# The first block's softmax: each component's negated maximum goes straight to its exponential, component 1 first

## The chip, the core and the metric

The kernel runs on one core of one Trainium2 chip. The metric is the device time of one execution in microseconds; the figure compared is the median of several runs. The engines are PE (TensorE, matmuls), DVE (VectorE), ACT (ScalarE), POOL (GpSimd) and SP, which here only issues the weight loads. They run side by side and wait for each other through semaphores.

## The reference

The program applies a first block and then a second block, each two layers deep, to x of 1024 tokens by 1024 features. Only the attention of the first block matters here. It has four heads; each head has two components c of 64 columns and one shared set of values of 128 columns. Rotation (RoPE) is applied to q and k.

```
q = q * (A_QK_DIM ** -0.5)
sc = jnp.einsum('bhcqd,bhckd->bhcqk', qi, kh)
p = jax.nn.softmax(jnp.where(mask, sc, NEG_INF), axis=-1)
w = p[:, :, 0] - lam * p[:, :, 1]
return jnp.einsum('bhqk,bhkv->bhqv', w, vh)
```

The result of a head is normalised (rms_norm), multiplied with silu(z), and later merged with a convolution branch and a retention branch. Queries are taken in blocks of 128, and block q of a head needs the keys 0 to 128(q+1).

## The kernel before, in words

Every engine has its own instruction stream, written out in the same order of steps; there is no scheduler. Attention of one layer (`attention` of each engine) runs over four heads h and eight query blocks q. The work of one block has these steps:

- PE `scores` (L728) computes both components' scores of 128 x 128(q+1) into the two buffers of psA; the last matmul of each component (L733) adds the causal mask and fills the buffer. It runs one block ahead, and may start when both buffers were drained by the exponentials of the block before.
- DVE `maxima` (L1274, L1275) takes the row maximum of each component and multiplies both with -SCALE (1/8), into `negmax`.
- ACT `exps` (L992) computes exp(SCALE * score + negmax) of each component into tiles 4 to 7 of X, which is free in that phase, with the row sum on the side; finishing it drains the score buffer.
- DVE `mix` (L1283 to L1285) takes the reciprocals of the sums, scales component 1 with its own and -lambda, and adds the scaled component 0.
- PE transposes the mixture (L706), ACT copies it (L1081), and PE multiplies it with the values (L778).

Between these, PE computes the projections of the next head (q, k, v, z, and in the last head the first panels of the convolution) as 24 matmuls of 128x512 for each half of the tokens (L483). These matmuls are most of PE's time in this phase. Each product is computed in three passes, with weights and activations split into a high and a low part; POOL splits each weight panel (L449, L452) once PE has begun the panel before.

Projections, transposes, rotations and the sum of squares of the head's output (L767) share three banks of psT in a ring called F. A step whose bank is still in use waits until the step three before it has been drained: q, k and v by ACT's copy (L1002), convolution panels by ACT's copy (L1011), the swapped q and k of the rotation by DVE's L1294, the sum of squares by ACT's logarithm (L1015). The order of each engine is fixed, so that L1002, L1011 and L1015 stand behind the exponentials of the next block on ACT, and L1294 behind the maxima of the next block on DVE. `B1_SLOTS` lists which step goes into which block; (("ss", 0, 0)) of block 6 puts L767 there, and ("v", 1, 1) of block 7 the projection that needs the bank of that sum.

`Ring` and `Tally` only count semaphores: `A.filled` is one semaphore for all of psA, counted in the order component 0, component 1; `A.drained` is one per buffer. `step` lets DVE wait for its own last instruction.

Of the kernel before, what the change touches and what calls it, by code (L numbers as in the profile page):

```python
# [19 lines left out]
ALU = mybir.AluOpType  # L20
ACT = mybir.ActivationFunctionType
AX_X = mybir.AxisListType.X
# [7 lines left out]
P = 128  # L30
SEQ, D_MODEL, DEPTH = 1024, 1024, 2
KT = D_MODEL // P
NT = SEQ // P
# [5 lines left out]
HEADS = 4  # L39
# [285 lines left out]
class C1:  # L325
# [5 lines left out]
    n = KT + 15  # L331


class C2:
# [13 lines left out]
    n = 100  # L348
# [3 lines left out]
class K:  # L352
# [11 lines left out]
    n = 896 + 1024 + 2  # L364
# [162 lines left out]
def first_block(env):  # L527
    nc, X, Hhi, Hlo, rope, ident, ones = env.nc, env.X, env.Hhi, env.Hlo, env.rope, env.ident, env.ones
    psA, psT, identb, maskb, epsc = env.psA, env.psT, env.identb, env.maskb, env.epsc
    SCALE = A_QK ** -0.5  # L530
    with ExitStack() as ctx:
        def sem(name):
            return env.sem("b1_" + name)

        def sb(name, shape, dt=F32):
            return ctx.enter_context(nc.sbuf_tensor("b1_" + name, shape, dt))
# [11 lines left out]
        lam = sb("lam", [P, 6])  # L548
# [1 line left out]
        swapa = sb("swapa", [P, P])  # L550
        swapr = sb("swapr", [P, P])
        rtab = sb("rtab", [P, K.n - K.dmask])
        rowmax = sb("rowmax", [P, 2])
        negmax = sb("negmax", [P, 2, 2])
        rowsum = sb("rowsum", [P, 2, 2])
        inv = sb("inv", [P, 2, 2])
# [4 lines left out]
        A = Ring("b1A", a_uses, env.sem)  # L561
# [3 lines left out]
        F = Ring("b1F", f, env.sem, 3)  # L565
# [8 lines left out]
        s, saved = env.s, env.saved  # L574
# [10 lines left out]
            sem(n) for n in ("sq2_done", "sq2_added", "summed2", "mean2", "root2", "both", "x_fin"))  # L585
        lam_sum, lam_exp = Tally(sem("lam_sum"), 1), Tally(sem("lam_exp"), 1)
        rotated = Tally(sem("rotated"), 4 * HEADS)
        nmax = Tally(sem("nmax"), HEADS * NT)
        mixed = Tally(sem("mixed"), HEADS * NT)
        a_sq, a_rs, a_out = (Tally(sem(n), 2 * HEADS) for n in ("a_sq", "a_rs", "a_out"))  # L590
        b_hi, b_lo = (Tally(sem(n), 2 * HEADS + 2 * B1_TILES) for n in ("b_hi", "b_lo"))
# [16 lines left out]
        TMP, ROT = upad[:, 2:2 + HALF], upad[:, 2 + HALF:]  # L608
# [364 lines left out]
        def scalar(act):  # L973
# [11 lines left out]
                act.activation(dst, psA[:, A.buf(use)], func).then_inc(A.freed(use), 1)  # L985

            def exps(L, h, q):
                act.wait_ge(*nmax.upto(L, h * NT + q + 1))
                n = (q + 1) * P
                for c in (0, 1):  # L990
                    use = ("s", h, q, c)
                    act.activation(PR[q % 2][c][:, 0:n], psA[:, A.buf(use), 0:n], ACT.Exp,  # L992
                                   bias=negmax[:, q % 2, c:c + 1], scale=SCALE,
                                   accum_out=rowsum[:, q % 2, c:c + 1]).then_inc(A.freed(use), 1)

            def piece(L, use):
# [259 lines left out]
        def vector(dve):  # L1256
            def step(ins):
                dve_step.step(dve, ins)
# [9 lines left out]

            def maxima(L, h, q):
                n = (q + 1) * P  # L1270
                for c in (0, 1):
                    use = ("s", h, q, c)
                    dve.wait_ge(*A.filled(L, use))
                    step(dve.reduce_max(rowmax[:, c:c + 1], psA[:, A.buf(use), 0:n], AX_X))  # L1274
                dve.tensor_scalar(negmax[:, q % 2], rowmax[:], -SCALE, None, ALU.mult).then_inc(nmax.sem, 1)  # L1275

            def mix(L, h, q):

                n = (q + 1) * P
                p0, p1 = PR[q % 2][0][:, 0:n], PR[q % 2][1][:, 0:n]  # L1280
                dve.wait_ge(*A.drained(L, ("s", h, q, 0)))
                dve.wait_ge(*A.drained(L, ("s", h, q, 1)))
                step(dve.reciprocal(inv[:, q % 2], rowsum[:, q % 2]))  # L1283
                step(dve.tensor_scalar(p1, p1, inv[:, q % 2, 1:2], lam[:, 4:5], ALU.mult, ALU.mult))
                dve.scalar_tensor_tensor(out=p0, in0=p0, scalar=inv[:, q % 2, 0:1], in1=p1, op0=ALU.mult, op1=ALU.add)\  # L1285
                    .then_inc(mixed.sem, 1)

            def piece(L, use):
                kind, h, half = use
                c, psF = slice(half * HALF, (half + 1) * HALF), bank(use)  # L1290
                if kind in ("sq", "sk"):
                    dst = (AQ if kind == "sq" else AK)[h % 2][:, c]
                    dve.wait_ge(*F.filled(L, use))
                    dve.tensor_tensor(ROT, psF, rope[:, 1, c], ALU.mult).then_inc(F.freed(use), 1)  # L1294
                    step(dve.tensor_tensor(dst, dst, rope[:, 0, c], ALU.mult))
                    dve.wait_ge(*F.drained(L, use))
                    dve.tensor_tensor(dst, dst, ROT, ALU.add).then_inc(rotated.sem, 1)
                    dve.wait_ge(*rotated.upto(L, rotations(h, kind[1], half)))
                elif kind == "vt":
                    dve.wait_ge(*F.filled(L, use))  # L1300
                    dve.tensor_copy(AVAL[h % 2][:, c], psF).then_inc(F.freed(use), 1)
                elif kind == "ss":
                    n = 2 * h + half
                    dve.wait_ge(*a_rs.upto(L, n + 1))
                    dve.scalar_tensor_tensor(out=TMP, in0=psAV, scalar=gcol[:, 0:1], in1=TMP, op0=ALU.mult,
                                             op1=ALU.mult).then_inc(AV.freed((h, half)), 1)
                    dve.wait_ge(*AV.drained(L, (h, half)))
                    dve.wait_ge(*F.drained(L, ("z", h, half)))
                    dve.tensor_tensor(TMP, TMP, Z[:, c], ALU.mult).then_inc(a_out.sem, 1)
# [1447 lines left out]
```

## Time and profile before

| | us |
|---|---|
| median of 3 runs | 3851.65 (3850.85 to 3853.29) |
| the profiled execution's own time | 3852.72 |
| its span | 3850.9 |
| PE busy | 3701.6 (96%) |
| DVE busy | 1759.4 (46%) |
| ACT busy | 1107.3 (29%) |
| POOL busy | 1408.3 (37%) |

Attention of the first block runs from about 88 to 415 us in the first layer, and from about 1265 to 1590 us in the second. In a row of a timeline stand the start, the duration, the engine, the line and the operation, what it writes and reads, and how many instructions were merged into the row; a bracket gives the idle time of the engine before it and the engine and line that ended it. In a row of the windows stand the stretch, its length, the busy time (and instructions) of PE, of PE's weight loads, of DVE, ACT and POOL, then the granted clock, the share of the DMA engines and GB/s. Granted clock is the share of full speed that TensorE was allowed. Line numbers are those of the kernel before; in the changed kernel the lines up to the maxima stand one lower, and in `mix` and `piece` they differ by up to three.

### The profile page before, as it was taken

To read this page: it belongs to the slowest core of one execution; us is meant where nothing else is said; L and a number is where in the kernel's file an instruction comes from. 1 tells how busy PE (TensorE), PEld (TensorE's weight loads), DVE (VectorE), ACT (ScalarE), POOL (GpSimd) and SP (SyncE) were. 2 spreads that over 40 slices of the span, in tenths; PEclk is the share of its full clock that TensorE was granted. 3 is DMA by queue.
4 is the path that set the end of the run, shared out by engine and by line. 5 is a ranking of instruction groups with operands and counts; after the bars stand their busy time and mean duration, and the time that the engine had idled before them with its cause. 6 is when DMAs were issued, how large, how long until landed. Compare 5 with 4: busy or idle time off the path is not lost.

```text
span 3850.9 us, 43042 instructions
## 1 busy us (share of the span) xinstructions
PE 3701.6 (96%) x16664; PEld 2832.3 (74%) x16664; DVE 1759.4 (46%) x2125; ACT 1107.3 (29%) x1819; POOL 1408.3 (37%) x734
## 2 busy tenths in 40 slices
PE   6999999999999999999999999999899999999999
PEld 5666788887778666788887787777666678766667
DVE  4555113223145655204213235882566579345654
ACT  3334100112212333210102212123455331435542
POOL 2212344343356222244442347442323255333324
PEclk9999999999999999999999999999899999999999
DMA  4000111111124100111111114311111231111122
GB/s 151 28 27 28 47 53 46 49 47 33 39 88 142 33 28 28 44 51 48 47 52 33 33 44 139 104 39 33 37 29 31 80 122 50 33 32 33 34 70 90
DMA packets 74684, 209.40 MB, mean 54 GB/s; under 512 B 8224, under 2 KB 13600, under 8 KB 74016
## 3 DMA queue, kind: packets, MB, share of 16 engines
q1 hardware_dynamic: 53712, 159.15, 14.0%
q10 hardware_dynamic: 20816, 48.01, 3.5%
q8 instruction: 118, 1.93, 0.2%
q14 instruction: 38, 0.31, 0.0%
HBM read 186.16 MB, written 20.97 MB: 54 GB/s over the span
## 4 chain that ended last, share of the span: by engine, by line
PE 88%; DVE 8%; ACT 3%; issue 1%; DMA 0%; SPq 0%; ACTq 0%; DVEq 0%
PE psA L502 45%; PE psT L483 17%; PE psA L483 7%; PE psA L1819 3%; PE psA L728 2%; PE psT L1886 2%; PE psT L778 2%; PE psT L1790 1%; PE psT L1795 1%; DVE b_rowmax L1274 1%; PE psT L1863 1%; ACT X L992 1%; PE psT L1860 1%; PE psT L706 1%; PE psT L700 1%
## 5 line engine op out<-in xcount | busy, mean ns | idle before, releaser
L449 POOL TENSOR_TENSOR Whi<-stage,credit 128x1024 fp32r<-128x1024 f32 (+2 forms) x364 | 600.6, 1650 | 2394.8 <-PE psA L502 1200.0
L452 POOL TENSOR_TENSOR Wlo<-stage,Whi 128x1024 fp32r<-128x1024 f32 (+2 forms) x364 | 807.4, 2218 | 28.6
L502 PE MATMUL psA<-Hhi,Whi 128*128 128x512 f32 x2240 | 702.6, 395 | 0.4 <-DVE b_ypad L2327 0.4
L502 PE MATMUL psA<-Hlo,Whi 128*128 128x512 f32 x2240 | 690.2, 389 | 0.0
L502 PE MATMUL psA<-Hhi,Wlo 128*128 128x512 f32 x2240 | 689.9, 389 | 0.0
L502 PEld LDWEIGHTS psA<-Hhi,Whi 128*128 128x128 f32 x2240 | 419.2, 188 | 101.3 <-issue 16.6
L502 PEld LDWEIGHTS psA<-Hlo,Whi 128*128 128x128 f32 x2240 | 420.5, 188 | 88.1
L502 PEld LDWEIGHTS psA<-Hhi,Wlo 128*128 128x128 f32 x2240 | 420.5, 188 | 88.1
L483 PE MATMUL psT<-Hhi,Whi 128*128 128x512 f32 x1024 | 426.9, 417 | 33.1 <-ACT b_upad L1015 15.0
L483 PE MATMUL psT<-Hhi,Wlo 128*128 128x512 f32 x1024 | 406.5, 397 | 0.0
L483 PE MATMUL psT<-Hlo,Whi 128*128 128x512 f32 x1024 | 406.5, 397 | 0.0
L483 PEld LDWEIGHTS psT<-Hhi,Whi 128*128 128x128 f32 x1024 | 197.6, 193 | 91.2 <-issue 51.3
L2337 DVE SCALAR_TENSOR_TENSOR b_wk<-b_ypad,b_cur,b_wk 128x1024 f32<-128x1024 f32 x120 | 230.5, 1921 | 4.1
L483 PEld LDWEIGHTS psT<-Hhi,Wlo 128*128 128x128 f32 x1024 | 196.7, 192 | 43.7
L483 PEld LDWEIGHTS psT<-Hlo,Whi 128*128 128x128 f32 x1024 | 197.6, 193 | 39.4 <-issue 3.2
L483 PE MATMUL psA<-Hhi,Whi 128*128 128x512 f32 x448 | 181.9, 406 | 7.2 <-DVE Hlo L1379 6.3
L483 PE MATMUL psA<-Hhi,Wlo 128*128 128x512 f32 x448 | 176.6, 394 | 0.0
L483 PE MATMUL psA<-Hlo,Whi 128*128 128x512 f32 x448 | 176.2, 393 | 0.0
L985 ACT ACTIVATE b_wk<-psA 128x1024 f32<-128x1024 f32 x44 | 45.1, 1026 | 443.1 <-PE psA L502 443.0
L1274 DVE TENSOR_REDUCE b_rowmax<-psA 128x1 f32<-128x256 f32 (+7 forms) x128 | 97.0, 757 | 165.2 <-PE psA L733 162.7
L1102 ACT ACTIVATE b_wk<-psA 128x1024 f32<-128x1024 f32 x32 | 32.9, 1027 | 440.8 <-PE psA L502 440.8
L1819 PE MATMUL psA<-b_wk 128*128 128x512 f32 (+3 forms) x384 | 149.4, 499 | 5.0 <-ACT b_wk L2076 4.5
(320 smaller groups left out, 4883.4 us busy)
## 6 DMA issues: line engine op xcount, KB each, us to landing
stage<-in_w SPq DMA_DIRECT2D x232, 512.0 KB, 3.5
stage<-in_w SPq DMA_DIRECT2D x68, 256.0 KB, 2.6
xs<-X ACTq DMA_DIRECT2D x8, 2048.0 KB, 8.0
stage<-in_w SPq DMA_DIRECT2D x32, 384.0 KB, 3.1
b_wk<-xs ACTq DMA_DIRECT2D x36, 256.0 KB, 5.2
rope<-in_ropes ACTq DMA_DIRECT2D x4, 1024.0 KB, 5.0
stage<-in_w SPq DMA_DIRECT2D x32, 128.0 KB, 2.1
X<-xs ACTq DMA_DIRECT2D x8, 512.0 KB, 8.1
```

What stands on the lines that cost most here:

```text
L449: pool.tensor_tensor(Whi[:, b, 0:n], stage[:, b, 0:n], credit[:, 0:1].broadcast_to([P, n]), ALU.add).then_inc(s.w_hi, 1)
L452: pool.tensor_tensor(Wlo[:, b, 0:n], stage[:, b, 0:n], Whi[:, b, 0:n].bitcast(F32), ALU.subtract).then_inc(s.w_split, 1)
L483: mm = pe.matmul(dst[0:M], w[:, cols], r[k][:, c], start=k == 0 and w is whi and r is rhi, stop=k == nk - 1 and end)
L502: mm = pe.matmul(dst[h], w[:, cols], r[k][:, h * HALF:(h + 1) * HALF], start=first and k == order[0] and r is rhi and w is whi, stop=last ...
L700: mm = pe.matmul(dst[:, c], lhsT, rhs[:, c], start=start, stop=stop)
L728: pe.matmul(dst[:, k0:k1], AQ[h % 2][rows, q * P:n], AK[h % 2][rows, k0:k1], start=True, stop=k1 < n)
L778: mm = pe.matmul(psAV[:, c0:], AVAL[h % 2][:, k * P:(k + 1) * P], WT[:, k, c0:], start=k == 0, stop=k == 4 * g + 3)
L985: act.activation(dst, psA[:, A.buf(use)], func).then_inc(A.freed(use), 1)
L1274: step(dve.reduce_max(rowmax[:, c:c + 1], psA[:, A.buf(use), 0:n], AX_X))
L1819: pe.matmul(dst[:, k0:k1], Q[sd][:, q * P:n], keys[g][:, 0:k1 - k0], start=True, stop=k1 < n)
L1886: mm = pe.matmul(psAV[side_rows(sd), c0:], v[:, b * M_V:(b + 1) * M_V], WT[sd][:, k, c0:], start=k == 0, stop=k == 4 * g + 3)
L2337: ins = dve.scalar_tensor_tensor(out=YC[:, t], in0=ypad[:, t, k:k + SEQ], scalar=col(C2.conv_w + 2 * k + t), in1=YC[:, t], op0=ALU.mult, o ...
```

## The change

`negmax` gets one maximum per component directly: the reduction is told to negate its result. The multiplication with SCALE moves from there and from the exponential to the rotation of q, whose two multiplications (by the sine and the cosine table) become scalar_tensor_tensor operations with SCALE as their constant; those of k get the same operations with 1.0. The tile `rowmax` and the instruction L1275 go. The semaphore `nmax` counts each component. Maxima and exponentials take component 1 first, and each exponential waits only for its own maximum. Both maxima wait until component 1's scores are filled, which come last. `mix` first waits for component 1, takes its reciprocal and scales it, and then waits for component 0 and takes that reciprocal by itself.

```diff
-        nmax = Tally(sem("nmax"), HEADS * NT)
+        nmax = Tally(sem("nmax"), 2 * HEADS * NT)
...
             def exps(L, h, q):
-                act.wait_ge(*nmax.upto(L, h * NT + q + 1))
                 n = (q + 1) * P
-                for c in (0, 1):
+                for c in (1, 0):
                     use = ("s", h, q, c)
+                    act.wait_ge(*nmax.upto(L, 2 * (h * NT + q) + 2 - c))
                     act.activation(PR[q % 2][c][:, 0:n], psA[:, A.buf(use), 0:n], ACT.Exp,
-                                   bias=negmax[:, q % 2, c:c + 1], scale=SCALE,
+                                   bias=negmax[:, q % 2, c:c + 1],
...
             def maxima(L, h, q):
                 n = (q + 1) * P
-                for c in (0, 1):
+                for c in (1, 0):
                     use = ("s", h, q, c)
-                    dve.wait_ge(*A.filled(L, use))
-                    step(dve.reduce_max(rowmax[:, c:c + 1], psA[:, A.buf(use), 0:n], AX_X))
-                dve.tensor_scalar(negmax[:, q % 2], rowmax[:], -SCALE, None, ALU.mult).then_inc(nmax.sem, 1)
+                    dve.wait_ge(*A.filled(L, ("s", h, q, 1)))
+                    dve.reduce_max(negmax[:, q % 2, c:c + 1], psA[:, A.buf(use), 0:n], AX_X, negate=True)\
+                        .then_inc(nmax.sem, 1)
...
             def mix(L, h, q):
-                dve.wait_ge(*A.drained(L, ("s", h, q, 0)))
-                dve.wait_ge(*A.drained(L, ("s", h, q, 1)))
-                step(dve.reciprocal(inv[:, q % 2], rowsum[:, q % 2]))
-                step(dve.tensor_scalar(p1, p1, inv[:, q % 2, 1:2], lam[:, 4:5], ALU.mult, ALU.mult))
+                dve.wait_ge(*A.drained(L, ("s", h, q, 1)))
+                step(dve.reciprocal(inv[:, q % 2, 1:2], rowsum[:, q % 2, 1:2]))
+                step(dve.tensor_scalar(p1, p1, inv[:, q % 2, 1:2], lam[:, 4:5], ALU.mult, ALU.mult))
+                dve.wait_ge(*A.drained(L, ("s", h, q, 0)))
+                step(dve.reciprocal(inv[:, q % 2, 0:1], rowsum[:, q % 2, 0:1]))
                 dve.scalar_tensor_tensor(out=p0, in0=p0, scalar=inv[:, q % 2, 0:1], in1=p1, op0=ALU.mult, op1=ALU.add)\
                     .then_inc(mixed.sem, 1)
...
                 if kind in ("sq", "sk"):
-                    dve.tensor_tensor(ROT, psF, rope[:, 1, c], ALU.mult).then_inc(F.freed(use), 1)
-                    step(dve.tensor_tensor(dst, dst, rope[:, 0, c], ALU.mult))
+                    scale = SCALE if kind == "sq" else 1.0
+                    dve.scalar_tensor_tensor(out=ROT, in0=psF, scalar=scale, in1=rope[:, 1, c], op0=ALU.mult,
+                                             op1=ALU.mult).then_inc(F.freed(use), 1)
+                    step(dve.scalar_tensor_tensor(out=dst, in0=dst, scalar=scale, in1=rope[:, 0, c], op0=ALU.mult,
+                                                  op1=ALU.mult))
```

DVE before, from the rotation in block 6 of head 0 to the mixing of block 7 (b1_dve_step is DVE's own step, b1A_filled the scores, b1A0_drained and b1A1_drained the two exponentials; psT holds the swapped k, X the exponentials):

```order
L1294 TENSOR_TENSOR b_upad<-psT,rope 128x512 [waits b1F_filled]
L1295 TENSOR_TENSOR b_wk<-b_wk,rope 128x512
L1297 TENSOR_TENSOR b_wk<-b_wk,b_upad 128x512 [waits b1F2_drained,b1_dve_step]
L1283 RECIPROCAL b_inv<-b_rowsum 128x2 [waits b1A1_drained,b1A0_drained,b1_rotated]
L1284 TENSOR_SCALAR X<-X,b_inv,b_lam 128x896 [waits b1_dve_step]
L1285 SCALAR_TENSOR_TENSOR X<-X,b_inv 128x896 [waits b1_dve_step]
L1274 TENSOR_REDUCE b_rowmax<-psA 128x1 [waits b1A_filled]
L1274 TENSOR_REDUCE b_rowmax<-psA 128x1 [waits b1A_filled,b1_dve_step]
L1275 TENSOR_SCALAR b_negmax<-b_rowmax 128x2 [waits b1_dve_step]
L1283 RECIPROCAL b_inv<-b_rowsum 128x2 [waits b1A1_drained,b1A0_drained]
L1284 TENSOR_SCALAR X<-X,b_inv,b_lam 128x1024 [waits b1_dve_step]
L1285 SCALAR_TENSOR_TENSOR X<-X,b_inv 128x1024 [waits b1_dve_step]
```

DVE after, the same stretch:

```order
L1295 SCALAR_TENSOR_TENSOR b_upad<-psT,rope 128x512 [waits b1F_filled]
L1297 SCALAR_TENSOR_TENSOR b_wk<-b_wk,rope 128x512
L1300 TENSOR_TENSOR b_wk<-b_wk,b_upad 128x512 [waits b1F2_drained,b1_dve_step]
L1281 RECIPROCAL b_inv<-b_rowsum 128x1 [waits b1A1_drained,b1_rotated]
L1282 TENSOR_SCALAR X<-X,b_inv,b_lam 128x896 [waits b1_dve_step]
L1284 RECIPROCAL b_inv<-b_rowsum 128x1 [waits b1A0_drained,b1_dve_step]
L1285 SCALAR_TENSOR_TENSOR X<-X,b_inv 128x896 [waits b1_dve_step]
L1273 TENSOR_REDUCE b_negmax<-psA 128x1 [waits b1A_filled] x2
L1281 RECIPROCAL b_inv<-b_rowsum 128x1 [waits b1A1_drained]
L1282 TENSOR_SCALAR X<-X,b_inv,b_lam 128x1024 [waits b1_dve_step]
L1284 RECIPROCAL b_inv<-b_rowsum 128x1 [waits b1A0_drained,b1_dve_step]
L1285 SCALAR_TENSOR_TENSOR X<-X,b_inv 128x1024 [waits b1_dve_step]
```

The negation after the maxima is gone, the two maxima no longer wait for DVE's own step, and a second reciprocal stands between the scaling and the mixing.

ACT before, at the end of head 0 (psA are the scores, L1002 copies a projection, L1081 the transposed mixture of block 6, L1015 is the logarithm of the sum of squares):

```order
L992 ACTIVATE X,b_rowsum<-psA,b_negmax 128x1024 [waits b1_nmax]
L992 ACTIVATE X,b_rowsum<-psA,b_negmax 128x1024
L1002 ACTIVATE b_wk<-psT 128x512 [waits b1F_filled]
L1081 ACTIVATE X<-psT 128x4x128 [waits b1F_filled]
L1081 ACTIVATE X<-psT 128x3x128 [waits b1F_filled]
```

ACT after, the same place:

```order
L991 ACTIVATE X,b_rowsum<-psA,b_negmax 128x1024 [waits b1_nmax] x2
L1001 ACTIVATE b_wk<-psT 128x512 [waits b1F_filled]
L1080 ACTIVATE X<-psT 128x4x128 [waits b1F_filled]
L1080 ACTIVATE X<-psT 128x3x128 [waits b1F_filled]
```

The order of ACT is the same but for the components; the second exponential now has a wait of its own. PE's instructions and waits are the same in both kernels, except that both counts of drained buffers come in the other order.

## Rows read from the trace of the kernel before

**Rows 1.** The page: busy time by engine, and the chain by engine

```profile
PE 3701.6 (96%) x16664; PEld 2832.3 (74%) x16664; DVE 1759.4 (46%) x2125; ACT 1107.3 (29%) x1819; POOL 1408.3 (37%) x734
...
PE 88%; DVE 8%; ACT 3%; issue 1%; DMA 0%; SPq 0%; ACTq 0%; DVEq 0%
```

**Rows 2.** Waits of PE: total us, times, longest us

```profile
PE psT L483 <- ACT b_upad L1015: 15.0, 10, 3.0
...
PE psT L483 <- DVE b_upad L1294: 9.4, 6, 1.6
PE psT L767 <- ACT b_wk L1002: 7.9, 6, 1.3
...
PE psA L728 <- ACT X L992: 5.1, 2, 2.6
...
PE psT L767 <- ACT b_wk L1011: 2.6, 2, 1.3
...
PE psT L706 <- DVE X L1285: 1.6, 8, 0.2
```

**Rows 3.** Timeline, all engines, first layer, end of head 0: start, us, engine

```profile
146.30 2.48 DVE L1274 TENSOR_REDUCE b_rowmax<-psA 128x1 f32<-128x1024 f32 x2 [4.19 <-PE psA L733]
...
148.66 2.39 POOL L452 TENSOR_TENSOR Wlo<-stage,Whi 128x1024 fp32r<-128x1024 f32 x1
...
148.82 2.25 DVE L1275 TENSOR_SCALAR b_negmax<-b_rowmax 128x2 f32<-128x2 f32 x1
...
153.30 0.59 ACT L1002 ACTIVATE b_wk<-psT 128x512 f32<-128x512 f32 x1
...
153.95 1.13 PE L767 MATMUL psT<-b_upad,ones 128*128 128x512 f32 x2 [1.31 <-ACT b_wk L1002]
154.56 1.28 DVE L1285 SCALAR_TENSOR_TENSOR X<-X,b_inv 128x1024 f32<-128x1024 f32 x1
...
155.43 0.28 PE L733 MATMUL psA<-maskb,identb 128*128 128x128 bf16 x2
155.76 0.61 DVE L1274 TENSOR_REDUCE b_rowmax<-psA 128x1 f32<-128x128 f32 x2
155.90 1.09 PE L706 MATMUL psT<-ident,X 128*128 128x128 f32 x8 [0.19 <-DVE X L1285]
...
156.60 0.37 ACT L992 ACTIVATE X<-psA,b_negmax 128x128 f32<-128x128 f32 x1 [1.85 <-DVE b_negmax L1275]
...
158.13 0.47 PE L483 MATMUL psT<-Hhi,Whi 128*128 128x512 f32 x1 [1.14 <-ACT b_upad L1015]
```

**Rows 4.** Timeline of PE, start of attention in the first layer

```profile
90.22 0.94 PE L728 MATMUL psA<-b_wk 64*128 64x256 f32 x4 [2.47 <-ACT X L992]
```

**Rows 5.** Timeline of DVE, block 6 of head 0

```profile
137.55 0.17 DVE L1275 TENSOR_SCALAR b_negmax<-b_rowmax 128x2 f32<-128x2 f32 x1
137.63 0.68 DVE L1294 TENSOR_TENSOR b_upad<-psT,rope 128x512 f32<-128x512 f32 x1
...
138.23 0.68 DVE L1295 TENSOR_TENSOR b_wk<-b_wk,rope 128x512 f32<-128x512 f32 x1
```

**Rows 6.** Groups of DVE by form, 80 to 420 us: busy us, mean ns

```profile
L1294 DVE TENSOR_TENSOR b_upad<-psT,rope 128x512 f32<-128x512 f32 x12 | 8.2, 685 | 0.0
...
L1305 DVE SCALAR_TENSOR_TENSOR b_upad<-psT,b_gcol,b_upad 128x512 f32<-128x512 f32 x8 | 6.0, 752 | 34.5 <-ACT b_upad L1017 34.5
```

**Rows 7.** Timeline, head 1, block 4

```profile
193.86 1.68 DVE L1274 TENSOR_REDUCE b_rowmax<-psA 128x1 f32<-128x640 f32 x2 [0.67 <-PE psA L733]
...
195.78 0.79 ACT L992 ACTIVATE X<-psA,b_negmax 128x640 f32<-128x640 f32 x1 [3.63 <-DVE b_negmax L1275]
...
198.17 0.47 PE L483 MATMUL psT<-Hhi,Whi 128*128 128x512 f32 x1 [2.99 <-ACT b_upad L1015]
```

**Rows 8.** Windows at the first and the second head boundary: granted clock third last

```profile
155.00:157.00 2.00, 1.80 (x15) 1.27 (x14) 1.50 (x4) 0.40 (x3) 0.00 (x0) 1.00 0.00 0
...
239.00:241.00 2.00, 1.61 (x5) 1.36 (x5) 1.02 (x2) 1.85 (x4) 0.00 (x0) 0.57 0.00 0
```

More of the change, by code:

```diff
@@ L552, in first_block @@
         rtab = sb("rtab", [P, K.n - K.dmask])
-        rowmax = sb("rowmax", [P, 2])
         negmax = sb("negmax", [P, 2, 2])
```

## The prediction

> **What bounds the kernel now.** I read the page first. TensorE is busy 96% of the span, and the chain that ended last runs 88% through PE, 8% through DVE and 3% through ACT [rows 1]. So nothing that merely shortens DVE or ACT work pays; a gain must remove time in which PE stands. The second view is PE's own list of waits [rows 2]. Six of its entries belong to first-block attention and come from the lines of the change or from instructions queued behind them: PE waits for ACT's L1015 (15.0 us in 10 waits), for ACT's L1002 (7.9 us in 6), for the exponentials L992 (5.1 us in 2), for ACT's L1011 (2.6 us in 2) and for the mixing L1285 (1.6 us in 8); DVE's L1294 adds 9.4 us in 6. That is 41.6 us, and no gain of the first order can exceed it. The third view is the timeline of all engines where a head ends and the next begins [rows 3]; I go through it below, since most of the money is there.
>
> I write M for a row maximum, N for the negation L1275, E for an exponential with its sum, and 0 and 1 for the components.
>
> **How the chain changes.** Before, E0 starts after M0, M1 and N. After, E1 starts when M1 ends, and M0 runs beside E1. E0 is late only if M0 takes longer than E1, and the rows have them nearly equal (for 1024 columns two M in 2.48, two E in the 2.23 between the end of N at 151.07 and ACT's next instruction at 153.30 [rows 3]). So at each place where PE waits for something behind the pair of exponentials one M and one N leave the chain. A cost comes with it: M1 starts only when component 1's mask matmul is done, 0.1 us after component 0's (two in 0.28 us [rows 3]).
>
> **The head boundary, three per layer.** At 148.82 N took 2.25 us instead of 0.17, as a GpSimd instruction (L452, 148.66 to 151.05) was running [rows 3]. Then came two E (151.07 to 153.30), ACT's copy L1002, and PE's L767 at 153.95 after 1.31 us idle. After the change M1 starts at 146.4 and ends at 147.65, E1 lasts to 148.9, M0 ends at 148.9, E0 at 150.2. L1002 then waits no longer for ACT: it copies what PE finishes at about 151.85, and ends at 152.5. PE is ready for L767 at 152.64, so the whole 1.31 goes. What is late next? The mixing. Its scaling L1284 is issued at 149.1 and may be held to 151.05, as N was; before, 1.26 us passed from the last exponential (153.30) to the start of L1285 (154.56), for a reciprocal and the scaling; 151.05, 1.26 and 1.28 for L1285 give 153.6. PE wants it after the mask matmuls, which move from 155.43 to 154.12, ending 154.40. So 0.8 us to spare, so the 0.19 before L706 goes too. Next M1 of the new head starts at 154.45; E1 follows 0.35 later, where it was 0.84 after the first M (155.76 to 156.60). From the first E to PE's L483 were 1.53 us (156.60 to 158.13), so L483 starts at 156.33. It was 158.13: 1.80 us, with 0.9 us of idle time left, since PE is ready at 154.4 + 1.09 = 155.5. Three boundaries: 5.4 us per layer.
>
> The Trainium skill, "SBUF — State Buffer", section on SBUF's two separate sides, calls the pair of ports that VectorE and GpSimd share an exclusive lock, held for the whole instruction. The long N agrees with that, 2.25 against 0.17 us [rows 3]. The rule speaks against a part of the hope: the scaling that now comes early would meet the same lock. The 153.6 above has that in it; without it mixing would end near 152.6, and the sum would be the same, as PE comes at 154.4.
>
> **The start of attention, once per layer.** PE idles 2.47 us for the first pair of exponentials [rows 4]. The maxima there are started by DVE, so the mask matmul costs nothing: 0.84 becomes 0.35, a gain of 0.49.
>
> **The waits for L1294, three per layer.** L1294 stands on DVE behind both maxima. N leaves, but N started at 137.55 and L1294 already at 137.63, since neither waits for the other [rows 5]: N was worth 0.08, not 0.17. Two maxima without waits between them may also start sooner, as L1295 starts 0.60 after L1294 though that lasts 0.68 [rows 5], where waited steps start after the end. Two such places give 0.2. Against it: 0.1 for the mask matmul, and 0.07 since L1294 becomes a scalar_tensor_tensor (L1305, the same size out of PSUM, has 752 ns; L1294 has 685 [rows 6]). Net +0.1 each, 0.3 per layer; bounds -0.1 and +0.15 each.
>
> The Trainium skill, "VectorE: DVE Perf Modes", section "The DRAIN you can't avoid", says that a semaphore after each VectorE op costs nothing over none. By it this term would be -0.1 each, and the total 1.2 us smaller. The 0.60 against 0.68 speaks against the rule here.
>
> **The waits of 2.98 us, two per layer.** At 193.86 two M of 0.84, then E at 195.78, then PE's L483 at 198.17, 2.39 later, behind L1015 [rows 7]. Now M1 starts at 193.97, E1 at 194.85, and E0 waits at most 0.05 for M0: 0.9 each, 1.8 per layer.
>
> **The last head, once per layer.** The wait for L1011, 1.31 us [rows 2], has the boundary's pattern, with exponentials that now end over 2 us sooner: all of it goes, 1.3.
>
> **What the change adds.** One reciprocal per block (0.17 and its wait 0.03) takes the place of N in DVE's total. The rotation's two multiplications each cost 0.07 more, 16 times per layer: 2.2 us of DVE per layer, behind which stand the mixing and the next maxima. DVE is busy 46% [rows 1]; only in block 3 of the first head does PE wait for the mixing, 0.22 us (one of the 8 of L1285 [rows 2]). There 0.07 + 0.20 come on top: -0.25 per layer. If that cover were absent everywhere else too, 0.25 on some 30 blocks would cost 8 us per layer; but PE does not stand for the mixing in any other block inside a head, so I take none. No row has a maximum with negation; the nearest are M itself and N. I take M's price; the upper bound is M plus N's 0.17 for each. No row has an exponential with the default scale; I take E.
>
> **Clock.** The granted clock is 1.00 at the first boundary, and 0.57 in the stretch from 239 to 241 at the second [rows 8], that is mostly at 1.2 GHz instead of 2.4; PE had idled 1.31 and 0.19 us and run short matmuls just before. Five of the six boundaries show it. It costs about 0.65 us each after L483 has begun: 0.43 of 2 us, less the share that was idle. With most idle time gone the fall may stay away: from 0 to +3.2 us in all. I take the middle, 1.6.
>
> **Sum.** Per layer 5.4 + 0.5 + 0.3 + 1.8 + 1.3 - 0.25 = 9.05; two layers 18.1; with the clock 19.7 us. PE bounds what follows, and the starts of other engines and of weight loads follow PE's panels, so the gain is kept. The profiled span of 3850.9 becomes 3831.2, its run's 3852.72 becomes 3833.0; the median lies 1.07 below that run: 3832.
>
> **Rivals.**
> - Half the gain. PE's next wait eats part of it: L1002's copy, or a bank freed late, keeps the boundary's first 1.31, and ACT's two separate waits cost 0.1 per block. For it: PE would have L767's bank only 0.05 us before it asks. Against: even then most of the idle time behind the new head's exponentials goes. Six times 1.3 fewer, and ten times 0.1: 3841.
> - No effect. The early E1 helps nobody, as what really holds the boundary is the GpSimd instruction and it moves its hold to L1284. Then the mixing would end at 153.6 only if E0 is on time; if E0 came late too, all boundaries stay, and what is left is start, last head and the waits of 2.98: at most 7.2 us, below 0.2% of the time: 3845 to 3850. Against: ACT does not use the held instruction's result for either exponential.
> - Slower. The negating maximum runs at half of M's rate. The place is DVE ahead of L1294: two M of 1.1 more at six waits are +13 us. At the four waits of 2.98 the chain M1, M0, E0 is 4.1 against 3.5: +2.4. In each head's block 3 DVE, which PE waits for already in the first, has up to 1.4 more work before the mixing: six times, +8.4. Starts and last heads still give 3.6, the boundaries perhaps 1.5 each, 9. Sum +11: 3863. On a line between -19.7 at M's duration and +11 at twice that, the change turns into a loss from about 1.65 times M. Nothing in the rows hints at it.
> - More. All falls of the clock stay away and PE, arriving sooner, draws GpSimd's splits out of the way of more DVE work: 3827.
>
> **Chances.** The forecast 0.68, half the gain 0.13, no effect 0.08, slower 0.04, more 0.07. A change of 0.2% (7.7 us) is about what a measurement of this kernel can tell. Faster by more, 0.88; within, 0.08; slower, 0.04. The range for 8 in 10 is 3826 to 3842: its upper end takes in the half gain, its lower end the clock's full 3.2 and the bound of the L1294 term.
>
> **What would show it.** In the changed profile: PE's waits for L1002 and L1011 (now one line number lower) gone; those of 2.98 near 2.1; L1294's successor nearly unchanged at 1.5 each; about 0.9 idle before L483 at each boundary; negating maxima of the same duration as M; scalings L1282 at the head's last block lengthened to about 2 us by GpSimd while no exponential waits for them; granted clock 1.00 around the boundaries. Wrong would be: idle time before L767 left over, or a maximum over 1.1 times M.

## The result, and the profile after

| | before | changed |
|---|---|---|
| median, us | 3851.26 (3850.85 to 3853.29, 4 runs) | 3825.89 (3822.25 to 3831.95, 4 runs) |
| ratio | | 0.9932 (0.992 to 0.9944) |
| profiled span, us | 3850.9 | 3825.6 |

The change makes the kernel 25.4 us faster; 19.7 were forecast, and the median lies 0.1 us below the forecast range. The page of the changed kernel answers to [rows 1]; first the busy times, then the chain by engine:

```profile
PE 3693.1 (97%) x16664; PEld 2826.3 (74%) x16664; DVE 1758.1 (46%) x2125; ACT 1110.1 (29%) x1819; POOL 1408.8 (37%) x734
...
PE 90%; DVE 6%; ACT 3%; issue 1%; DMA 0%; SPq 0%; ACTq 0%; DVEq 0%
```

DVE has hardly less work (1758.1 against 1759.4 us), but less of it is on the chain: 6% instead of 8%. PE's waits after, to be held against [rows 2] (all lines are one lower or, for the rotation, one higher):

```profile
PE psT L483 <- ACT b_upad L1014: 14.0, 10, 2.0
...
PE psT L483 <- DVE b_upad L1295: 7.8, 6, 1.3
...
PE psA L727 <- ACT X L991: 3.7, 2, 1.8
...
PE psT L705 <- DVE X L1285: 0.8, 2, 0.4
```

The waits for L1001 and L1010 (L1002 and L1011 before) are gone from the list; the mixing is waited for twice instead of eight times. The waits for the norm's logarithm are still ten, but now six of 1.0 and four of 2.0 us. The six waits of attention that the prediction added up to 41.6 us are 26.3 us now, 15.3 less. That is not the whole gain, because PE's own busy time fell too, by 8.5 us: fewer of its matmuls ran at half clock (the mean granted clock of the execution is 0.990 instead of 0.988). The first wait of attention in the first layer, as [rows 4]:

```profile
89.27 0.70 PE L727 MATMUL psA<-b_wk 64*128 64x256 f32 x4 [1.84 <-ACT X L991]
```

The end of head 0 in the first layer, all engines, as [rows 3]:

```profile
145.07 0.28 PE L732 MATMUL psA<-maskb,identb 128*128 128x128 bf16 x2
...
145.40 2.35 DVE L1273 TENSOR_REDUCE b_negmax<-psA 128x1 f32<-128x1024 f32 x2 [4.36 <-PE psA L732]
...
146.65 1.12 ACT L991 ACTIVATE X<-psA,b_negmax 128x1024 f32<-128x1024 f32 x1 [1.50 <-DVE b_negmax L1273]
...
147.70 2.39 POOL L452 TENSOR_TENSOR Wlo<-stage,Whi 128x1024 fp32r<-128x1024 f32 x1
...
147.78 1.12 ACT L991 ACTIVATE X<-psA,b_negmax 128x1024 f32<-128x1024 f32 x1
...
147.89 0.17 DVE L1281 RECIPROCAL b_inv<-b_rowsum 128x1 f32<-128x1 f32 x1
...
148.09 2.55 DVE L1282 TENSOR_SCALAR X<-X,b_inv,b_lam 128x1024 f32<-128x1024 f32 x1
...
150.88 1.28 DVE L1285 SCALAR_TENSOR_TENSOR X<-X,b_inv 128x1024 f32<-128x1024 f32 x1
150.95 0.60 ACT L1001 ACTIVATE b_wk<-psT 128x512 f32<-128x512 f32 x1 [1.96 <-PE psT L483]
...
151.60 1.12 PE L766 MATMUL psT<-b_upad,ones 128*128 128x512 f32 x2
...
153.20 1.04 PE L705 MATMUL psT<-ident,X 128*128 128x128 f32 x8
...
153.73 0.37 ACT L991 ACTIVATE X<-psA,b_negmax 128x128 f32<-128x128 f32 x1 [1.31 <-DVE b_negmax L1273]
...
155.26 0.47 PE L483 MATMUL psT<-Hhi,Whi 128*128 128x512 f32 x1 [1.01 <-ACT b_upad L1014]
```

Read it by its waits. Component 1's exponential starts 1.25 us after the first maximum (146.65), and component 0's follows without a gap. ACT now waits for PE before L1001, where PE waited for ACT. GpSimd holds the scaling L1282, for 2.55 us, as it held the negation for 2.25 in [rows 3]; but the mixture is ready at 152.16 and PE comes for it at 153.20. From the mask matmul of block 7 to PE's L483 behind the boundary it is now 10.19 us (145.07 to 155.26). Before, the mask matmul stood at 146.03 and L483 at 158.13 [rows 3], 12.10 us. So a boundary gave 1.91, where 1.80 were forecast. The row for 146.03, in the timeline before:

```profile
146.03 0.28 PE L733 MATMUL psA<-maskb,identb 128*128 128x128 bf16 x2
```

PE runs the same matmuls in the same order in both kernels, so the start of each can be compared between the traces. Inside attention the changed kernel gets ahead by 0.6 us at the start of the first layer and 0.8 at that of the second, by 0.27 at each wait for the rotation, 1.9 at each boundary (2.5 where the clock had fallen before), 1.0 at each wait of the 2.98 kind and 1.4 at the last head, and falls back by 0.19 in block 3 of the first head. A fall of the clock at 1360 us takes 1.6 back. Otherwise the distance stays the same inside attention.

### The profile page after: what moved, and what is told of

Its sections match the earlier page's. It is cut to its first block, busy times and chain, and to the rows that moved or that the text cites. A ratio compares the mean times of both kernels' runs of the same rounds, so it can differ in the third digit from the quotient of the medians.

```text
span 3825.6 us, 42998 instructions
## 1 busy us (share of the span) xinstructions
PE 3693.1 (97%) x16664; PEld 2826.3 (74%) x16664; DVE 1758.1 (46%) x2125; ACT 1110.1 (29%) x1819; POOL 1408.8 (37%) x734
## 4 chain that ended last, share of the span: by engine, by line
PE 90%; DVE 6%; ACT 3%; issue 1%; DMA 0%; SPq 0%; ACTq 0%; DVEq 0%
PE psA L502 45%; PE psT L483 18%; PE psA L483 7%; PE psA L1822 3%; PE psA L727 2%; PE psT L1889 2%; PE psT L777 2%; PE psT L1793 1%; PE psT L1798 1%; PE psT L705 1%; PE psT L1866 1%; PE psT L1863 1%; PE psT L699 1%; DVE Hlo L2317 1%; DVE b_wk L2340 1%
## 5 line engine op out<-in xcount | busy, mean ns | idle before, releaser
L483 PE MATMUL psT<-Hhi,Whi 128*128 128x512 f32 x1024 | 425.3, 415 | 30.5 <-ACT b_upad L1014 14.0
L483 PE MATMUL psT<-Hhi,Wlo 128*128 128x512 f32 x1024 | 405.4, 396 | 0.0
L483 PE MATMUL psT<-Hlo,Whi 128*128 128x512 f32 x1024 | 404.5, 395 | 0.0
L483 PEld LDWEIGHTS psT<-Hhi,Whi 128*128 128x128 f32 x1024 | 196.5, 192 | 87.6 <-issue 48.1
L483 PEld LDWEIGHTS psT<-Hhi,Wlo 128*128 128x128 f32 x1024 | 195.4, 191 | 43.4
L483 PEld LDWEIGHTS psT<-Hlo,Whi 128*128 128x128 f32 x1024 | 196.8, 192 | 39.3 <-issue 3.2
L483 PE MATMUL psA<-Hhi,Whi 128*128 128x512 f32 x448 | 181.6, 405 | 7.3 <-DVE Hlo L1382 6.1
L1273 DVE TENSOR_REDUCE b_negmax<-psA 128x1 f32<-128x256 f32 (+7 forms) x128 | 91.0, 752 | 187.7 <-PE psA L732 187.6
L483 PE MATMUL psA<-Hlo,Whi 128*128 128x512 f32 x448 | 176.0, 393 | 0.0
L483 PE MATMUL psA<-Hhi,Wlo 128*128 128x512 f32 x448 | 175.8, 392 | 0.0
```

Of the source, the lines that this page charges most:

```text
L483: mm = pe.matmul(dst[0:M], w[:, cols], r[k][:, c], start=k == 0 and w is whi and r is rhi, stop=k == nk - 1 and end)
L1273: dve.reduce_max(negmax[:, q % 2, c:c + 1], psA[:, A.buf(use), 0:n], AX_X, negate=True)\
```

## The experiments

Times are medians; e1 to e4 shared nine runs of the kernel before (3850.7), e5 to e8 another nine (3849.7). "Attention" is the time in us from the start of the first mask matmul of a layer to the start of its last L767, from the profiled execution; the tail is what follows the start of the last L767 of the second layer.

| | time | ratio (95%) | attention | tail |
|---|---|---|---|---|
| before | 3851.26 | | 327.9, 328.7 | 2257.9 |
| changed | 3825.89 | 0.9932 (0.992 to 0.9944) | 316.4, 317.9 | 2255.9 |
| e1 changed again | 3824.74 | 0.9934 (0.992 to 0.9947) | 316.2, 319.5 | 2251.1 |
| e2 no negation only | 3832.75 | 0.9951 (0.9937 to 0.9964) | 319.7, 319.6 | 2255.9 |
| e3 order only | 3831.16 | 0.9947 (0.9934 to 0.9961) | 320.4, 322.1 | 2251.6 |
| e4 dummy in block 7 | 3825.66 | 0.9933 (0.992 to 0.9947) | 317.5, 317.5 | 2251.1 |
| e5 norm step first | 3808.91 | 0.9893 (0.9877 to 0.9908) | 308.1, 308.1 | 2255.7 |
| e6 joint mixing | 3823.18 | 0.9936 (0.9922 to 0.9949) | 316.2, 316.1 | 2251.1 |
| e7 scale in the copy | 3824.89 | 0.9935 (0.9921 to 0.9948) | 316.4, 319.5 | 2251.1 |
| e8 e5, e7 and own masks | 3809.13 | 0.9896 (0.988 to 0.9911) | 308.0, 308.0 | 2256.2 |
| e9 before, again | 3853.52 (one run) | | 329.6, 331.1 | 2254.6 |
| e10 before, again | 3854.60 (one run) | | 328.8, 328.8 | 2258.5 |
| e11 changed, again | 3822.31 (one run) | | 316.4, 316.3 | 2251.3 |

**e1: the changed kernel again.** No edit.

> The changed kernel once more, unchanged. Attention alone gave 11.9 us in the first layer and 11.3 in the second in the profiled execution; 2.1 us of its gain lie behind the last attention, where nothing was edited. Theory A (the waits and the five falls of the clock at head boundaries make the gain, the rest is chance): the median lies 22 to 26 us below the kernel before, the single runs spread by about 10 us as in the first four (3822.25 to 3831.95), and the spans go with the mean granted clock (higher clock, shorter span). Theory B (the time behind attention is a real effect of the change): 25 or more, with the same 2 us behind the last attention in the new trace.

26.0 us below the kernel before, which is at the edge of A and inside B, so the median does not decide; the runs go from 3822.51 to 3829.66, a spread of 7.2 us against 9.7 of the first four. The stretch behind attention was 4.8 us shorter than in the first trace of the same kernel. So single executions differ there by nearly as much as the forecast missed by (5.7); B's "same 2 us" became 6.8.

**e2: only the negation goes.**

```diff
-                for c in (1, 0):
+                act.wait_ge(*nmax.upto(L, 2 * (h * NT + q) + 2))
+                for c in (0, 1):
...
-                    act.wait_ge(*nmax.upto(L, 2 * (h * NT + q) + 2 - c))
...
-                for c in (1, 0):
+                for c in (0, 1):
...
-                    dve.wait_ge(*A.filled(L, ("s", h, q, 1)))
+                    dve.wait_ge(*A.filled(L, use))
...
-                step(dve.reciprocal(inv[:, q % 2, 1:2], rowsum[:, q % 2, 1:2]))
+                dve.wait_ge(*A.drained(L, ("s", h, q, 0)))
+                dve.wait_ge(*A.drained(L, ("s", h, q, 1)))
+                step(dve.reciprocal(inv[:, q % 2], rowsum[:, q % 2]))
```

> Only the negation goes: negated maxima, SCALE in the rotation of q, but component 0 first, both exponentials behind both maxima, one reciprocal for both components as before. Theory A (at a boundary it is the held negation of 2.25 us that costs; elsewhere the maximum that runs beside an exponential): boundaries gain 1.65 us each instead of 1.9, the last heads all of 1.31, the four waits of 2.98 only 0.3 instead of 1.0, the starts 0.3 instead of 0.9; the falls of the clock at the boundaries stay away. Sum 15.8 without the clock, about 19 with it. Theory B (the early exponential of component 1 makes the gain at the boundary too): under 9 us in all.

18.0 us of the 26.0, where about 19 were expected from A and under 9 from B. PE's waits:

```profile
PE psT L483 <- ACT b_upad L1014: 17.5, 10, 2.7
...
PE psT L483 <- DVE b_upad L1294: 7.5, 6, 1.2
...
PE psA L727 <- ACT X L991: 4.3, 2, 2.1
```

The waits for L1001 are gone here too, without any exponential moved ahead of a maximum. At the first boundary e2 gains 1.78 us where the changed kernel gains 1.91, so nearly all of it is the negation that GpSimd held. At the 2.98 waits only 0.3 us went (2.7 left), so the other 0.7 there are the order. At the starts about 0.4 of 0.7 us came without the order. The waits for the rotation fell as in the changed kernel (7.5 us; with the order alone, in e3, they rise to 10.1).

**e3: only the order.** The rotation and SCALE are as in the kernel before. The lines below are set against the kernel before, of `exps` and `maxima` only the ones that matter; there is now one tensor_scalar per component:

```diff
-                for c in (0, 1):
+                for c in (1, 0):
...
-                dve.tensor_scalar(negmax[:, q % 2], rowmax[:], -SCALE, None, ALU.mult).then_inc(nmax.sem, 1)
+                    dve.tensor_scalar(negmax[:, q % 2, c:c + 1], rowmax[:, c:c + 1], -SCALE, None, ALU.mult)\
+                        .then_inc(nmax.sem, 1)
```

> Only the order: component 1 first, each exponential behind its own maximum, the mixing split, but maxima still negated and scaled by a tensor_scalar, now one of 128x1 per component; rotation as before. Theory A: a tensor_scalar of one element per partition is held by GpSimd as the one of two was, so at block 7 the two are held up to the ends of GpSimd's two instructions (148.6 and 151.05 in the time of before); the boundary gains about 1.2, the waits of 2.98 about 0.75 each, starts 0.5, waits for the rotation nothing; in all 13 to 16 us with the clock. Theory B (the order makes the gain): 20 us or more.

19.5 us: above A's 13 to 16 and just below B's 20. A missed here, and the timeline says why:

```profile
146.15 1.89 POOL L449 TENSOR_TENSOR Whi<-stage,credit 128x1024 fp32r<-128x1024 f32 x1 [13.88 <-PE psT L483]
...
147.07 0.15 DVE L1275 TENSOR_SCALAR b_negmax<-b_rowmax 128x1 f32<-128x1 f32 x1
...
147.15 1.22 DVE L1274 TENSOR_REDUCE b_rowmax<-psA 128x1 f32<-128x1024 f32 x1
...
148.12 2.39 POOL L452 TENSOR_TENSOR Wlo<-stage,Whi 128x1024 fp32r<-128x1024 f32 x1
...
148.39 0.15 DVE L1275 TENSOR_SCALAR b_negmax<-b_rowmax 128x1 f32<-128x1 f32 x1
```

Both negations ran for 0.15 us in the middle of a GpSimd instruction. The trace has 22 of them that started inside one, and all took 0.15 us. In the kernel before, 12 of the 64 negations of two columns started inside one: the eight of block 7 took 2.25 us, four others in the last heads 1.13 to 1.36, and each ended with the GpSimd instruction, to 0.03 us. The other 52 took 0.17. So a tensor_scalar of one column per partition is not held, and one of two columns is. So e3 also takes the hold away, and e2 and e3 overlap: 18.0 and 19.5 do not add up to 26.0, because either of them frees the boundary. What the order alone does not free is the rotation, which now stands behind one more negation:

```profile
PE psT L483 <- DVE b_upad L1296: 10.1, 6, 1.7
```

**e4: a held dummy put back in block 7.**

```diff
-                    dve.reduce_max(negmax[:, q % 2, c:c + 1], psA[:, A.buf(use), 0:n], AX_X, negate=True)\
-                        .then_inc(nmax.sem, 1)
+                    last = dve.reduce_max(negmax[:, q % 2, c:c + 1], psA[:, A.buf(use), 0:n], AX_X, negate=True)
+                    if q == NT - 1:
+                        step(last)
+                        last = dve.tensor_scalar(tok[:, 0, 2 * c:2 * c + 2], lam[:, 2:4], 1.0, None, ALU.mult)
+                    last.then_inc(nmax.sem, 1)
```

> The changed kernel with a dummy tensor_scalar of 128x2 in SBUF (it writes a tile that nothing reads) between each maximum and its signal, in block 7 of each head alone. If an instruction that GpSimd holds is what cost the boundary and the last head, then the dummies run to about 2 us where they meet L452, the idle time before L766 comes back in part (0.3 to 0.6 us of the former 1.31), and the time rises by 3 to 6 us over the changed kernel, 8 boundaries and last heads in all; with falls of the clock coming back up to 9. If the hold did not matter, the dummies cost their 0.17 each beside the exponential and under 1 us in all.

```profile
145.96 0.99 DVE L1276 TENSOR_SCALAR b_tok<-b_lam 128x2 f32<-128x2 f32 x1
...
147.00 2.40 POOL L452 TENSOR_TENSOR Wlo<-stage,Whi 128x1024 fp32r<-128x1024 f32 x1
...
148.11 1.32 DVE L1276 TENSOR_SCALAR b_tok<-b_lam 128x2 f32<-128x2 f32 x1
```

```profile
PE psT L766 <- ACT b_wk L1001: 1.3, 6, 0.2
...
PE psT L766 <- ACT b_wk L1010: 0.4, 2, 0.2
```

With two columns the hold is back, 0.99 and 1.32 us, and so for all 16 dummies. The idle time before L766 is back in place and number, but 0.2 us each, because the dummies end with the two GpSimd instructions. PE falls behind the changed kernel by 0.23 to 0.34 us at each of the eight places, 2.3 us in all; the medians differ by 0.9 (3825.66 against 3824.74), which is not clear of the noise. The place was right, the price of 3 to 6 us was too high.

**e5: the norm's logarithm ahead of the exponentials.** The profile after left 14.0 us behind L1014, so its place on ACT was tried.

```diff
+                        for use in late:
+                            piece(L, use)
                         if q + 1 < NT:
                             exps(L, h, q + 1)
                         elif h + 1 < HEADS:
                             exps(L, h + 1, 0)
-                        for use in late:
-                            piece(L, use)
```

> The changed kernel, with one step of ACT moved: the logarithm and exponential for the head's norm (L1014, L1016) stand ahead of the next block's score exponentials instead of behind them. If the 14.0 us that PE still waits for L1014 in 10 waits (1.0 at each boundary, 2.0 at the four others) are set only by its place behind the exponentials (theory A), they go, as its input is there over 1 us before the first maximum is: the time falls by 12 to 15 us against the changed kernel, to about 3811. If ACT is short of time there (theory B: the exponentials then start 1.3 us later and the next wait of PE for them or for the mixing takes it back), it falls by under 5 us.

3808.91: 40.8 us below its kernel before, 15 below the changed kernel (40.8 less 25.4 to 26.0). All ten waits for L1014 are gone from PE's list. At the first boundary:

```profile
152.27 0.69 ACT L1014 ACTIVATE b_upad<-psT,epsc 128x512 f32<-128x512 f32 x1 [0.35 <-PE psT L766]
...
152.99 0.63 ACT L1016 ACTIVATE b_upad<-b_upad 128x512 f32<-128x512 f32 x1
153.51 0.48 PE L483 MATMUL psT<-Hhi,Whi 128*128 128x512 f32 x1
...
153.53 0.35 ACT L991 ACTIVATE X<-psA,b_negmax 128x128 f32<-128x128 f32 x1
```

L1014 runs while ACT had been idle, L483 has no idle time before it, and the exponential stands behind L1016; PE's waits for the exponentials are unchanged (3.7 us in 2).

**e6: the mixing as before the change.**

```diff
-                dve.wait_ge(*A.drained(L, ("s", h, q, 1)))
-                step(dve.reciprocal(inv[:, q % 2, 1:2], rowsum[:, q % 2, 1:2]))
+                dve.wait_ge(*A.drained(L, ("s", h, q, 0)))
+                dve.wait_ge(*A.drained(L, ("s", h, q, 1)))
+                step(dve.reciprocal(inv[:, q % 2], rowsum[:, q % 2]))
```

> The changed kernel with the mixing as before: it waits for both exponentials, takes both reciprocals at once and then scales. Theory A (PE comes to the mixture later than DVE in every block but block 3 of the first head, so scaling early is worth nothing): the time is that of the changed kernel, within 1 us; PE's wait for L1285 there falls from 0.4 to 0.2 us. Theory B (the early scaling is what makes the mixing ready at the boundaries): PE waits for the mixing 8 times again, and the time rises by 2 us or more.

3823.18, 26.5 us below its kernel before: no loss that can be told. The only wait of PE in attention that changed is the one expected:

```profile
PE psT L705 <- DVE X L1284: 0.4, 2, 0.2
```

So the early scaling gains nothing that can be told, and costs 0.2 us in block 3 of the first head of each layer.

**e7: SCALE in ACT's copy of q, plain multiplications.**

```diff
-                    act.activation(dst[:, c], psF, ACT.Copy).then_inc(F.freed(use), 1)
+                    act.activation(dst[:, c], psF, ACT.Copy, scale=SCALE if kind == "q" else 1.0)\
+                        .then_inc(F.freed(use), 1)
...
-                    scale = SCALE if kind == "sq" else 1.0
-                    dve.scalar_tensor_tensor(out=ROT, in0=psF, scalar=scale, in1=rope[:, 1, c], op0=ALU.mult,
-                                             op1=ALU.mult).then_inc(F.freed(use), 1)
...
+                    dve.tensor_tensor(ROT, psF, rope[:, 1, c], ALU.mult).then_inc(F.freed(use), 1)
...
```

> The changed kernel with SCALE applied by ACT's copy of q (its scale operand) and the rotation back at plain tensor_tensor. It sizes the term of the sum for scalar_tensor_tensor: 0.07 us at each of the six waits for the rotation and 0.14 in block 3 of the first heads, 0.7 us in all, too small for the timing; in the trace the waits fall from 1.30 to 1.23 us, and the two for the mixing from 0.41 to about 0.27. If it is more than 3 us, the longer rotations hold something that the waits of PE do not show.

The waits did not move: 7.8 us in 6, 1.3 each, and 0.8 in 2. So the term of 0.07 us was wrong, which the changed kernel's own groups show as well (by form, 80 to 410 us):

```profile
L1295 DVE SCALAR_TENSOR_TENSOR b_upad<-psT,rope 128x512 f32<-128x512 f32 x12 | 8.2, 682 | 0.2 <-PE psT L761 0.2
L1308 DVE SCALAR_TENSOR_TENSOR b_upad<-psT,b_gcol,b_upad 128x512 f32<-128x512 f32 x8 | 6.0, 752 | 33.0 <-ACT b_upad L1016 33.0
```

With a constant it takes 682 ns, where tensor_tensor took 685 [rows 6]; with a scalar read from a tile, 752. The median, 3824.89, lies between the two of the changed kernel.

**e8: candidate.** e5 and e7, and the mask matmuls in the order of the maxima:

```diff
-                for c in (0, 1):
+                for c in (1, 0):
                     dst = psA[:, A.buf(("s", h, q, c))]
...
-                    dve.wait_ge(*A.filled(L, ("s", h, q, 1)))
+                    dve.wait_ge(*A.filled(L, ("s", h, q, 1 - c)))
```

> A candidate for the fastest: the changed kernel with ACT's norm step ahead of the score exponentials, SCALE in the copy of q, and component 1's mask matmul before component 0's, so that each maximum waits for its own scores only. Theory A: the moved norm step gives 12 to 15 us, the scale 0.7, the mask matmul's 0.1 us about 20 times where it counts 1 to 2: 3808 to 3811. Theory B (short ACT): 3820 or above.

3809.13 (3808.58 to 3809.83), not to be told from e5. The waits for the rotation fell from 7.8 to 7.5 us in 6, 0.05 each, half of what the earlier mask was to give. The 0.7 us for the scale did not come, as in e7. e5, with one step moved, is enough.

**e9, e10, e11: both kernels once more, for their traces.**

> The kernel before, unchanged, for a second trace. Attention should last 327.9 and 328.7 us again (from the first mask matmul to the last L767), within 1.5 us each by falls of the clock. The stretch behind the last attention was 2257.9 us in the trace before, and 2255.9, 2251.1, 2255.9, 2251.6 and 2251.1 in traces of the changed kernel and of e1 to e4, which have the same code there. Theory A (chance of the clock): it takes one of these values here too, not always 2258. Theory B (the change shortens it): 2258 again in both traces of the kernel before.

> The kernel before once more, as e9: theory A, a stretch behind the last attention between 2251 and 2258 us; theory B, 2258.

> The changed kernel once more: attention 316.3 and 317.9 to 319.5 us; the stretch behind it between 2251 and 2258 by theory A, never over 2256 by theory B.

The tail of the kernel before was 2254.6 and 2258.5, so not always 2258; it overlaps with the 2251.1 to 2256.2 of the others (2255.9 in e2). That is for theory A. But the three tails of the kernel before average 2257.0, the three of the changed kernel 2252.8, with the same instructions; three against three do not settle whether those 4 us are luck. All ten traces of kernels other than the one before, which have the same code in the tail, average 2253.1. A part is the clock: worked out from the traces, the mean granted clock of the tail is 0.9859, 0.9846 and 0.9850 before and 0.9854, 0.9861 and 0.9869 in the changed kernel; over 2255 us that difference is 2 of the 4 us. Attention, on the other hand, is clear: six layers of before 327.9 to 331.1, mean 329.1; six of the changed kernel 316.2 to 319.5, mean 317.1; that is 12.0 per layer, 24.1 for both.

In e9 the falls of the clock stood elsewhere than in [rows 8]. None stood at a boundary. One came right behind PE's wait of 2.98 us in head 1, which ended at 197.17 (windows as in [rows 8]):

```profile
196.00:198.00 2.00, 0.83 (x4) 0.73 (x5) 0.28 (x1) 1.97 (x5) 0.00 (x0) 1.00 0.00 0
198.00:200.00 2.00, 2.00 (x7) 1.58 (x6) 1.97 (x4) 0.81 (x2) 0.00 (x0) 0.56 0.00 0
200.00:202.00 2.00, 2.00 (x7) 1.59 (x6) 1.89 (x5) 0.00 (x0) 0.00 (x0) 0.58 0.00 0
```

So the same wait is followed by a fall in one execution and not in another. In the three traces of before I count 7, 6 (one of them twice as long) and 7 falls in the two attentions, their starts included; in those of the changed kernel 3, 4 and 2; in e5 and e8, where PE waits least, 2 each. In all thirteen traces every fall inside attention began during one of three kinds of PE's waits, or at most 2.2 us behind it: the first wait of attention, a wait of 2.0 to 3.0 us before L483, or the 1.31 before L767 at a boundary. None came at a boundary of the changed kernel, where 1.0 us of waiting is left. A fall behind a wait of 1.98 us cost 1.6 us; one at a boundary cost 0.6, where PE's wait before L483 was shorter for it (0.4 instead of 1.14). That the waits bring the falls is what this suggests; no run changed the one without the other. In the changed kernel the window at the second boundary stands at full clock, and the one fall in mid-attention of its first trace follows a wait of 1.98 us:

```profile
233.00:235.00 2.00, 1.62 (x7) 1.39 (x8) 1.03 (x2) 1.84 (x4) 0.00 (x0) 1.00 0.00 0
1359.00:1361.00 2.00, 2.00 (x8) 1.59 (x9) 1.56 (x3) 0.94 (x3) 0.00 (x0) 0.77 0.00 0
1361.00:1363.00 2.00, 2.00 (x6) 1.57 (x5) 1.93 (x4) 0.55 (x1) 0.00 (x0) 0.50 0.00 0
```

## Why the prediction was off

The direction, the places and the kinds of wait were right; what failed are the sizes of single terms of the sum, the waits for the rotation and the clock above all, and a stretch that the sum left out. The time came out nearest to the rival "more" (3827), of whose two reasons one holds: the falls of the clock at the boundaries stayed away. That GpSimd's splits moved out of DVE's way is not seen; they hold L1282 as forecast. The terms were too small, nearly all of them. By its own steps:

- **Head boundary**, forecast 1.80: 1.91. The idle time of 1.31 went, the scaling was held as said (2.55 us), 1.01 was left where 0.9 was said. e2 shows that the held negation was nearly all of the price (1.78); the early exponential adds 0.13.
- **Start**, forecast 0.5: 0.6 in the first layer (PE's wait went from 2.47 to 1.84 us) and 0.8 in the second (2.59 to 1.85).
- **Waits of 2.98**, forecast 0.9: 1.0 (2.0 left).
- **Waits for the rotation**, forecast 0.1: 0.27 (1.57 to 1.30). This is the step with the largest relative error, and all of its smaller terms were off the same way. The 0.07 for scalar_tensor_tensor was taken from a row with a tile for a scalar, and is nothing with a constant (e7). The mask matmul costs 0.05 and not 0.1 (e8). And the two places without a wait give 0.24, not 0.2. Block 6 of head 0, as [rows 5]:

```profile
134.67 2.09 DVE L1273 TENSOR_REDUCE b_negmax<-psA 128x1 f32<-128x896 f32 x2 [1.74 <-PE psA L732]
...
136.68 0.68 DVE L1295 SCALAR_TENSOR_TENSOR b_upad<-psT,rope 128x512 f32<-128x512 f32 x1
```

  The rotation starts 2.01 us after the first maximum; before, it was 2.33 (135.30 to 137.63). The rule weighed in the prediction, from the Trainium skill, "VectorE: DVE Perf Modes", section "The DRAIN you can't avoid", that a semaphore costs nothing over none, fails here: 0.32 us, of which 0.08 are the negation's and 0.24 the missing waits'. The same section also says that a next instruction which is not held starts earlier, and with that the trace agrees.
- **Block 3 of the first head**, forecast -0.25: -0.19.
- **Last head**, forecast 1.3: 1.4.
- Together 10.4 per layer where 9.05 were forecast: 21 instead of 18.1 us. The waits for the rotation are 1.0 of these 3 us, the boundaries 0.7.
- **Clock**, forecast 1.6 as the middle between 0 and 3.2: by the mean of three traces each, 24.1 less 21 leaves about 3 us, its upper end. In the first pair of traces alone it was near the forecast: five falls at boundaries less, of 0.6 us each, and one fall of 1.6 more. The falls at boundaries stayed away in all traces of the changed kernel; one or two came behind waits of 1.98.
- **Outside attention**, forecast 0: 2.6 us between and behind the attentions in the first pair of traces. By the medians (25.4 and 26.0) less the 24.1 of attention it is 1 to 2, by the mean tails of three traces each 4. The prediction put it at nothing, on the ground that PE bounds what follows, so that the gain is kept as it is. Its size, and whether it belongs to the change, stay open.

So the miss of 5.7 us is 3 of mis-sized waits, 1.5 of clock and 1 to 2 outside attention. Of this the range's lower end had the full 3.2 of the clock and the bound of the rotation, 0.3; these two lead from 3832 to 3830, and the rest down to 3826 had no term behind it. So it is luck that the result lies only 0.1 us outside. The extra reciprocal and the split mixing were rightly put at nothing outside block 3 (e6).

## What to carry to other kernels

Before an instruction is priced by its duration, look whether it ever was held: 52 of the 64 negations took 0.17 us, but the eight in block 7 took 2.25, on the path that PE waits for. When a step leaves a chain, look in the profile after for what now stands behind it for no reason: moving the norm's logarithm ahead of the exponentials (e5) brought another 15 us, more than half of what the whole change did, without changing an instruction. And give small terms bounds of their own, not only the large ones: here six errors of 0.06 to 0.3 us, all of one sign, made up half of the miss.

## What the runs showed of the hardware

- A tensor_scalar on SBUF of 128x2 f32 is held while GpSimd runs a tensor_tensor (2.25, 0.99, 1.32 us instead of 0.17; all 12 in the kernel before and all 16 in e4 that started inside one); of 128x1 it is not (0.15 us, all 22 in e3). A reciprocal is not held at 128x2 either: the 12 of L1283 that started inside one took 0.17 us in the kernel before. The Trainium skill, "SBUF — State Buffer", section on SBUF's two separate sides, names as holders and held a VectorE instruction in a 2-port mode; the holds above agree with that, and that one column does not count as such is what e3 adds.
- scalar_tensor_tensor of 128x512 with an immediate scalar: 682 ns; with a per-partition scalar 752.
- tensor_reduce with negated result: 1220 ns for 1024 columns, against 1224 without.
- The same kernel's execution varies by 7 to 10 us here (3822.25 to 3831.95; before, 3845.71 to 3853.54 on the second chip), and up to 4.8 us of that lie in unchanged code behind the last attention.
